# One decoder layer, MLA and NSA side by side: compression results in score banks, wo's splits and key pairs in the first attention, group norm gains in wo's split

## The chip, the cores and the metric

The kernel runs on one core of a Trainium2 chip. The metric is the time of one execution on the device in microseconds, the median of several runs. All times of a trace come from one profiled execution.

## What is computed

One layer for 512 positions of width 1024, in float32. After an RMS norm, one projection feeds two attentions, and both outputs go, each with its own RMS norm, through one matrix; then a squared-ReLU feed-forward part.

```python
h = rms_norm(x, ln1_g)
h_q, h_kv, h_kr, q_b, kv_b, gate_b = split(h @ w_in)
o_a = mla_mixer(...)      # 8 heads, causal, 512 keys, low-rank q and kv
# nsa_mixer: 8 heads, 2 kv heads, three branches with sigmoid gates
k_cmp = rms_norm(silu(blocks_k @ w1) @ w2, k_gain[0])   # 31 blocks of 32 positions
v_cmp = silu(blocks_v @ w1) @ w2
o_b = g0 * o_cmp + g1 * o_sel + g2 * o_win              # sel takes all 8 key blocks here
mix = concat([rms_norm(o_a, grp_norm_mla), rms_norm(o_b, grp_norm_nsa)])
x = x + mix @ w_o
h2 = rms_norm(x, ln2_g)
x = x + square(relu(h2 @ w_up)) @ w_down
```

## The kernel before

**Precision.** Dense products run as three matmuls of a faster 32-bit form: each operand is split into a rounded part and the rest (`hi`, `lo`), and hi·hi, hi·lo and lo·hi are added in PSUM. A weight piece is 128 x 1024; SyncE loads it into one of three `raw` buffers, ScalarE writes `w_hi` (L608), VectorE writes `w_lo = raw - w_hi` (L927). Both live in a ring of five. A raw buffer is free when its `w_lo` is written (`raw_free`), a ring slot when its last product has run. The order of the pieces is a list, `weight_pieces`: eight pieces of wo, the first five ahead of the four of `w1`, which are not split.

**Units.** Positions come in four tiles of 128, t = 0 to 3. An attention unit is one tile of queries of one head: scores (`score_unit`, two score banks `S`), minimum and subtraction on VectorE (`low_unit`, L1087), the exponential on ScalarE (L741), 128x128 turns by TensorE into one of two `T` banks (L1454), a copy out by ScalarE for even units and VectorE for odd ones (`pt_out`, L751 and L1097), and the product with the values (`mix_unit`, L1640). TensorE's order in step n is: scores of n, filling work, product of n-4, turn of n-2. The first attention has 32 units, n = 0 to 31; the second counts u = n - 32: sel 3 (u 0 to 7), win 3 (8 to 15), sel 2 (16 to 23), win 2 (24 to 31), cmp 3 (32), sel 1 (33 to 40), cmp 2 (41), win 1 (42 to 49), cmp 1 (50), sel 0, win 0, cmp 0 (67). A compression unit holds all eight heads.

**Filling work.** In the first attention: 32 projection pieces for the second attention's keys, values and gates, spread by `unit_of`, and the norms of its queries and keys (`NORM_AT`: squares on ScalarE, sums and two products on VectorE, turns). In the second, `compress(u)` of each engine: at u 0 to 9 the key taps, gates and bias are turned; at u 10 to 17 the hidden layer of the compression; at u 21, 23 and 27 its second products `kc` and `vc` and the turn of `kc`, which go into `T` banks, between the turns of the probabilities. `take` hands out the two banks of a kind in turn and makes TensorE wait until the user two before has been read. Mixed rows of the first attention (`mix_row_of` on GpSimd: norm factor, then gain row L563) are turned at u 19, 21, 23 and 25 and split by ScalarE and VectorE in the two units after. From u 28 on the products with wo (`WO_UNITS`) fill TensorE.

**What sets the order.** Each engine works its program strictly in order, and the positions are written out by hand: `WO_SPLIT` says in which unit of the second attention each piece of wo is split (4, 6, 7, 9, 9, 44, 45, 46), `PAIR_KEYS` and `PAIR_QUERIES` when keys and queries are put into hi/lo pairs (`pair_his`, `pair_los`), `X_AGAIN` after which piece SyncE loads x again. The keys of tile 3 are paired in the step after the first attention's last scores, ahead of its last output row. An output row (`out_row`) divides a branch's eight heads by their sums; the mix of the branch two later waits for it, as both share a bank `O`.

## Time and profile before

| | us |
|---|---|
| median of 3 runs | 725.37 (724.8 to 729.68) |
| the profiled execution | 724.78, span 722.5 |
| TensorE busy, of the span | 691.0 |
| VectorE busy | 366.6 |
| ScalarE busy | 292.8 |
| GpSimd busy | 107.6 |
| stages: input projections | 0 to 103 |
| first attention | 103 to 190 |
| second attention and wo | 190 to 378 |
| feed-forward | 378 to 722.5 |

A profile page names the engines PE (TensorE), DVE (VectorE), ACT (ScalarE), POOL (GpSimd) and SP (SyncE). A row of windows gives a stretch of time and its length, then how long each engine was busy in it, with its number of instructions, in the order TensorE's matmuls, TensorE's weight loads (beside the matmuls), VectorE, ScalarE, GpSimd; then the clock that TensorE was granted (1.00 is 2.4 GHz, 0.50 is 1.2 GHz), the share of the DMA engines and GB/s. A row of a group gives line, engine, operation, output and inputs with their shapes, how often, then the busy time in us and the mean of one in ns. A row of waits says which instruction's end released an engine that stood idle. A busy TensorE at half clock shows as busy.

### The profile page before, as it was taken

To read this page: it belongs to the slowest core of one execution; us is meant where nothing else is said; L and a number is where in the kernel's file an instruction comes from. 1 tells how busy PE (TensorE), PEld (TensorE's weight loads), DVE (VectorE), ACT (ScalarE), POOL (GpSimd) and SP (SyncE) were. 2 spreads that over 40 slices of the span, in tenths; PEclk is the share of its full clock that TensorE was granted. 3 is DMA by queue.
4 is the path that set the end of the run, shared out by engine and by line. 5 is a ranking of instruction groups with operands and counts; after the bars stand their busy time and mean duration, and the time that the engine had idled before them with its cause. 6 is when DMAs were issued, how large, how long until landed. Compare 5 with 4: busy or idle time off the path is not lost.

```text
span 722.5 us, 9978 instructions
## 1 busy us (share of the span) xinstructions
PE 691.0 (96%) x3703; PEld 590.8 (82%) x3703; DVE 366.6 (51%) x713; ACT 292.8 (41%) x630; POOL 107.6 (15%) x152
## 2 busy tenths in 40 slices
PE   7999999999899799898799999999999999999998
PEld 5989877888689788787699888888888888888886
DVE  4645665777685764767655454323224445432311
ACT  5554665556674542645244343321122343321110
POOL 2526654310240300224100000000000000000000
PEclk9999999999999899989999999999999999999999
DMA  7331314100245000020033322322322322322302
GB/s 281 115 130 33 117 61 149 62 27 2 88 154 206 22 1 0 15 74 31 1 117 100 104 88 94 110 88 96 109 88 88 115 89 87 114 91 88 103 1 102
DMA packets 18529, 62.14 MB, mean 86 GB/s; under 512 B 2184, under 2 KB 2312, under 8 KB 18482
## 3 DMA queue, kind: packets, MB, share of 16 engines
q1 hardware_dynamic: 17138, 57.50, 23.7%
q0 software_dynamic: 1200, 3.94, 1.7%
q8 instruction: 30, 0.49, 0.3%
q14 instruction: 17, 0.14, 0.1%
q10 hardware_dynamic: 144, 0.07, 0.0%
HBM read 59.35 MB, written 2.15 MB: 85 GB/s over the span
## 4 chain that ended last, share of the span: by engine, by line
PE 84%; DVE 7%; issue 3%; ACT 3%; DMA 1%; POOL 1%; SPq 0%; DVEq 0%; ACTq 0%; POOLq 0%
PE bank L1433 14%; PE bank L1435 14%; PE bank L1434 14%; PE bank L1756 8%; PE bank L1755 8%; PE bank L1754 8%; PE bank L1454 6%; PE bank L1640 5%; PE bank L1601 2%; PE bank L1682 1%; DVE w_lo L927 1%; DVE s_buf L1087 1%; DMA x<-x 1%; PE bank L1613 1%; PE bank L1612 1%
## 5 line engine op out<-in xcount | busy, mean ns | idle before, releaser
L927 DVE TENSOR_TENSOR w_lo<-raw,w_hi 128x1024 fp32r<-128x1024 f32 (+3 forms) x97 | 113.5, 1175 | 122.7 <-ACT w_hi L608 122.5
L608 ACT ACTIVATE w_hi<-raw 128x1024 fp32r<-128x1024 f32 (+3 forms) x97 | 97.5, 1011 | 122.5 <-PE bank L1435 118.2
L1754 PE MATMUL bank<-act_hi,w_hi 128*128 128x512 f32 (+3 forms) x288 | 106.8, 371 | 0.0
L1756 PE MATMUL bank<-act_hi,w_lo 128*128 128x512 f32 (+3 forms) x288 | 106.7, 370 | 0.0
L1755 PE MATMUL bank<-act_lo,w_hi 128*128 128x512 f32 (+3 forms) x288 | 106.7, 370 | 0.0
L1433 PE MATMUL bank<-w_hi,a_hi 128*128 128x512 f32 x256 | 99.6, 389 | 0.0
L1434 PE MATMUL bank<-w_lo,a_hi 128*128 128x512 f32 x256 | 99.6, 389 | 0.0
L1435 PE MATMUL bank<-w_hi,a_lo 128*128 128x512 f32 x256 | 99.6, 389 | 0.0
L1433 PE MATMUL bank<-w_hi,act_hi 128*128 128x512 f32 (+3 forms) x224 | 92.3, 412 | 2.5 <-DVE act_lo L940 2.3
L1434 PE MATMUL bank<-w_lo,act_hi 128*128 128x512 f32 (+3 forms) x224 | 81.4, 363 | 0.0
L1435 PE MATMUL bank<-w_hi,act_lo 128*128 128x512 f32 (+3 forms) x224 | 81.0, 362 | 0.0
L741 ACT ACTIVATE p_buf<-s_buf,stats 128x128 f32<-128x128 f32 (+3 forms) x96 | 53.5, 558 | 45.0 <-PE bank L1454 36.1
L1398 DVE TENSOR_TENSOR sq_b<-relu_b 128x512 f32<-128x512 f32 x32 | 22.1, 692 | 82.0 <-ACT relu_b L912 82.0
L912 ACT ACTIVATE relu_b<-bank 128x512 f32<-128x512 f32 x32 | 19.1, 598 | 106.3 <-PE bank L1756 106.3
L1755 PEld LDWEIGHTS bank<-act_lo,w_hi 128*128 128x128 f32 x288 | 54.2, 188 | 9.2
L1754 PEld LDWEIGHTS bank<-act_hi,w_hi 128*128 128x128 f32 x288 | 54.2, 188 | 9.0
L1756 PEld LDWEIGHTS bank<-act_hi,w_lo 128*128 128x128 f32 x288 | 54.2, 188 | 9.0
L1434 PEld LDWEIGHTS bank<-w_lo,a_hi 128*128 128x128 f32 x256 | 48.1, 188 | 10.0
L1433 PEld LDWEIGHTS bank<-w_hi,a_hi 128*128 128x128 f32 x256 | 48.1, 188 | 10.0
L1435 PEld LDWEIGHTS bank<-w_hi,a_lo 128*128 128x128 f32 x256 | 48.1, 188 | 9.9
L1433 PEld LDWEIGHTS bank<-w_hi,act_hi 128*128 128x128 f32 x224 | 43.4, 194 | 11.7 <-DVE act_lo L940 2.8
L1454 PE MATMUL bank<-consts,p_buf 128*128 128x128 f32 x248 | 45.7, 283 | 7.3 <-DVE kc_row L1310 3.5
(193 smaller groups left out, 1062.5 us busy)
## 6 DMA issues: line engine op xcount, KB each, us to landing
raw<-weights SPq DMA_DIRECT2D x86, 512.0 KB, 3.3
x<-x SPq DMA_DIRECT2D x8, 512.0 KB, 7.0
raw<-weights SPq DMA_DIRECT2D x7, 384.0 KB, 4.4
bias<-bias_by_distance POOLq DMA_DIRECT2D x1, 2048.0 KB, 9.1
y<-x SPq DMA_DIRECT2D x8, 256.0 KB, 2.2
raw<-weights SPq DMA_DIRECT2D x4, 288.0 KB, 2.8
raw<-weights SPq DMA_DIRECT2D x4, 280.0 KB, 3.0
consts<-consts SPq DMA_DIRECT2D x1, 688.0 KB, 4.1
```

The source lines that it names most:

```text
L608: act.activation(w_hi[:, m % RING, 0:width], raw[:, n % RAW, 0:width], ACT.Copy).then_inc(*hi_done.mark(n))
L741: act.activation(p_buf[:, n % 2, 0:nk], s_buf[:, n % 2, 0:nk], ACT.Exp, scale=-1.0, bias=neg_max[:, m:m + 1], accum_out=den[:, d:d + 1]).t ...
L927: dve.tensor_tensor(w_lo[:, m % RING, 0:width], raw[:, n % RAW, 0:width], w_hi[:, m % RING, 0:width].bitcast(F32), ALU.subtract).then_inc( ...
L1398: dve.tensor_tensor(sq_b[:, f % 2, :], relu_b[:, f % 2, :], relu_b[:, f % 2, :], ALU.mult).then_inc(*sq_done.mark((half, f)))
L1433: pe.matmul(dst, a_h, w_h, start=start, stop=False)
L1434: pe.matmul(dst, a_h, w_l, start=False, stop=False)
L1435: return pe.matmul(dst, a_l, w_h, start=False, stop=stop)
L1454: ins = pe.transpose(bank[0:m, i * step:i * step + k], tile, ident[0:k, 0:k])
L1640: ins = pe.matmul(bank[:, 64 * h:64 * h + 64], pt_buf[:, n % 2, j * P:(j + 1) * P], v, start=j == 0, stop=j == t)
L1754: pe.matmul(dst, h[:, ws], act_hi[:, k, cols], start=k == 0, stop=False)
L1755: pe.matmul(dst, h[:, ws], act_lo[:, k, cols], start=False, stop=False)
L1756: ins = pe.matmul(dst, l[:, ws], act_hi[:, k, cols], start=False, stop=k == KD - 1)
```

## The change

1. The weights' order: three pieces of wo ahead of w1, the other five behind; x is loaded again after the last piece of w1.
2. The splits of wo: pieces 0, 1, 2 in units 17, 27, 30 of the first attention; 3 to 7 at u 20, 29, 38, 40, 42.
3. The projection pieces of the first attention end two to three units sooner, so that the keys of tile 3 are paired at unit 29; query norms come at units 9, 16, 19, 22. The last query pair moves from u 43 to u 46.
4. The second products of the compression go into columns 384 to 511 of score bank `S[1]`, which units 16 to 31 leave free, ahead of the scores of u 19, 27 and 25; the score unit two later waits until VectorE has read them. `vc` is made once, for 32 rows, and copied to four places.
5. Mixed rows of the first attention are turned at u 9, 15, 20, 23. GpSimd norms the fourth after the compressed key's norm factor.
6. The gains of both group norms are multiplied into wo when it is split, as a scale per partition: each split is two ScalarE and two VectorE instructions of 512 columns. The gain rows, their load and the gain pass go.
7. Four tiles are zeroed by GpSimd before its eight loads of `tap_planes`, not by VectorE at u 6.

```diff
-    add("wo", RING, 1024)
+    add("wo", 3, 1024)
     add("w1", 4, 1024, False)
-    add("wo", 8, 1024, first=RING)
+    add("wo", 8, 1024, first=3)
...
-X_AGAIN = PIECE_AT["w1", 2]
+X_AGAIN = PIECE_AT["w1", 3]
...
-WO_SPLIT = {0: 4, 1: 6, 2: 7, 3: 9, 4: 9, 5: 44, 6: 45, 7: 46}
+WO_SPLIT = {0: 17 - N_MLA, 1: 27 - N_MLA, 2: 30 - N_MLA, 3: 20, 4: 29, 5: 38, 6: 40, 7: 42}
...
-    return 2 + (4 * row + piece_) * 30 // 32
+    return 2 + (4 * row + piece_) * 27 // 32
...
-NORM_AT = {ROW_END[0]: ("nkv", 0), 6: ("nq", 3), ROW_END[1]: ("nkv", 1), 10: ("nq", 2), ROW_END[2]: ("nkv", 2),
-           14: ("nq", 1), ROW_END[3]: ("nkv", 3), 19: ("nq", 0)}
+NORM_AT = {ROW_END[0]: ("nkv", 0), ROW_END[1]: ("nkv", 1), 9: ("nq", 3), ROW_END[2]: ("nkv", 2), ROW_END[3]: ("nkv", 3),
+           16: ("nq", 2), 19: ("nq", 1), 22: ("nq", 0)}
...
-PAIR_QUERIES = {25: 3, N_MLA + 13: 2, N_MLA + 23: 1, N_MLA + 43: 0}
+PAIR_QUERIES = {25: 3, N_MLA + 13: 2, N_MLA + 23: 1, N_MLA + 46: 0}
...
+MIX_AT = {9: 0, 15: 1, 20: 2, 23: 3}
+KC_AT, VC_AT, KT_AT = 19, 27, 25
+TAIL = 3 * P
+TAIL_READ = {KC_AT: "kc0", VC_AT: ("vd", 3), KT_AT: "k_cmp"}
...
+            pool.memset(v_diag, 0.0)
+            pool.memset(hid_v, 0.0)
+            pool.memset(hid_k, 0.0)
+            pool.memset(k_cmp, 0.0).then_inc(*pool_step.mark("zeros"))
             for h in range(HEADS):
...
-            for t in range(NT):
+            for t in range(3):
                 mix_row_of(0, t)
-            sum_branches("win", 3)
             pool.wait_ge(*dve_step.at("kc_ss"))
             rsqrt("kc", kc_rs[0:64, :], kc_ss[0:64, :], HD)
-            sum_branches("win", 2)
+            mix_row_of(0, 3)
+            for t in (3, 2):
+                sum_branches("win", t)
...
+                if PIECES[n][0] == "wo":
+                    for j, gain in enumerate(group_gains(n)):
+                        cols = slice(512 * j, 512 * j + 512)
+                        ins = dve.scalar_tensor_tensor(w_lo[:, m % RING, cols], raw[:, n % RAW, cols], gain,
+                                                       w_hi[:, m % RING, cols].bitcast(F32), ALU.mult, ALU.subtract)
...
-                        for g in range(2):
-                            rep = lambda v: v[:, g, :].unsqueeze(1).to_broadcast([P, 4, N_CMP])
-                            dve.tensor_tensor(hid_v[:, g, :, 0:N_CMP], rep(z), rep(r), ALU.mult).then_inc(*dve_step.mark(("hid_v", g)))
+                        dve.tensor_tensor(hid_v[:, :, 0:N_CMP], z, r, ALU.mult).then_inc(*dve_step.mark("hid_v"))
...
+                if u == KT_AT - 1:
+                    dve.wait_ge(*rsqrt_done.at("kc"))
+                    dve.scalar_tensor_tensor(kc_sq, kc_row, kc_rs[0:64, :], const("g_nk", 64)[:, 0:HD], ALU.mult, ALU.mult).then_inc(*dve_step.mark("kc2"))
...
+            def compress_tail(u):
+
+                if u == KC_AT:
+                    pe.wait_ge(*dve_step.at("hid_k"))
+                    pe.matmul(S[1][0:64, TAIL:TAIL + HD], hid_k, const("w2")[:, 0:HD], start=True, stop=True).then_inc(*turned.mark("kc"))
+                if u == VC_AT:
+                    pe.wait_ge(*dve_step.at("hid_v"))
+                    for g in range(2):
+                        ins = pe.matmul(S[1][0:NC, TAIL + g * HD:TAIL + (g + 1) * HD], hid_v[:, g, :], const("w2")[:, HD:], start=True, stop=True)
+                    ins.then_inc(*turned.mark("vc"))
+                if u == KT_AT:
+                    pe.wait_ge(*dve_step.at("kc2"))
+                    pe.transpose(S[1][0:64, TAIL:TAIL + 64], kc_sq, ident[0:64, 0:64]).then_inc(*turned.mark("kcT"))
...
+                if n - 2 - N_MLA in TAIL_READ:
+                    pe.wait_ge(*dve_step.at(TAIL_READ[n - 2 - N_MLA]))
+                compress_tail(n - N_MLA)
```

## Rows read from the trace of the kernel before

**Rows 1.** Windows by stage: length, busy us (count) per engine, granted clock, DMA.

```profile
145.00:190.00 45.00, 43.19 (x309) 37.31 (x308) 31.08 (x83) 25.36 (x66) 3.06 (x5) 1.00 0.02 9
190.00:212.00 22.00, 18.67 (x134) 15.16 (x133) 20.52 (x46) 18.27 (x42) 11.62 (x18) 1.00 0.45 145
236.00:262.00 26.00, 20.89 (x142) 19.57 (x141) 19.28 (x54) 13.90 (x36) 6.67 (x9) 0.87 0.00 1
300.00:316.00 16.00, 12.35 (x63) 10.39 (x63) 11.90 (x33) 9.66 (x24) 4.97 (x5) 0.79 0.25 81
378.00:722.50 344.50, 341.27 (x1544) 283.92 (x1543) 123.49 (x139) 94.66 (x123) 0.00 (x0) 1.00 0.28 92
```

**Rows 2.** Windows around the three longest stops, columns as before.

```profile
242.30:245.80 3.50, 0.03 (x1) 0.03 (x1) 3.47 (x8) 0.36 (x1) 1.54 (x2) 0.86 0.00 0
245.80:251.20 5.40, 5.40 (x25) 5.40 (x26) 1.92 (x6) 3.23 (x7) 0.72 (x2) 0.50 0.00 0
303.20:306.80 3.60, 0.39 (x5) 0.21 (x3) 3.31 (x9) 2.83 (x7) 0.00 (x0) 0.93 0.18 46
306.80:313.10 6.30, 6.30 (x22) 5.55 (x23) 3.04 (x9) 1.94 (x5) 2.15 (x4) 0.50 0.40 143
346.90:350.80 3.90, 1.29 (x12) 1.13 (x11) 2.52 (x4) 1.09 (x2) 0.00 (x0) 0.98 0.02 4
350.80:354.20 3.40, 3.40 (x8) 2.73 (x9) 3.15 (x10) 0.00 (x0) 0.00 (x0) 0.52 0.00 0
```

**Rows 3.** Waits of TensorE, 190 to 212: total us, times, longest.

```profile
PE bank L1454 <- DVE tap_planes L1251: 2.5, 3, 1.2
...
PE bank L1682 <- DMA raw<-weights: 0.5, 1, 0.5
```

**Rows 4.** Waits of TensorE, 236 to 262.

```profile
PE bank L1454 <- DVE kc_row L1310: 3.5, 1, 3.5
PE bank L1454 <- DVE v_diag L1320: 1.1, 1, 1.1
PE bank L1454 <- DVE k_cmp L1328: 0.6, 1, 0.6
```

**Rows 5.** Waits of TensorE, 300 to 316.

```profile
PE bank L1640 <- DVE o_nsa L1123: 3.2, 1, 3.2
```

**Rows 6.** VectorE's groups of instructions, 190 to 212: busy us, mean ns.

```profile
L927 DVE TENSOR_TENSOR w_lo<-raw,w_hi 128x1024 fp32r<-128x1024 f32 x5 | 6.3, 1281 | 0.0
...
L1271 DVE MEMSET v_diag<- 128x512 f32 x1 | 0.5, 485 | 0.1
```

**Rows 7.** VectorE in order of time, units 20 to 24: start, length.

```profile
238.44 0.55 DVE L1087 CUSTOM_DVE_ANT_0 s_buf<-bank,bias 128x384 f32<-128x384 f32 x1
...
238.91 0.17 DVE L1108 TENSOR_SCALAR stats<-stats 128x8 f32<-128x8 f32 x1
...
239.55 0.69 DVE L1131 TENSOR_TENSOR raw_row<-bank,stats 128x512 f32<-128x512 f32 x1
...
240.63 0.64 DVE L1293 TENSOR_SCALAR z_buf<-z_buf 128x62 f32<-128x62 f32 x1
...
241.88 2.11 DVE L1304 TENSOR_TENSOR hid_v<-z_buf 128x124 f32<-128x124 f32 x2
...
253.16 0.69 DVE L1211 TENSOR_TENSOR q_pairs<-n_q,q_pairs 64x512 fp32r<-64x512 f32 x1
```

**Rows 8.** TensorE in order of time: first score products of two units.

```profile
237.68 0.42 PE L1612 MATMUL bank<-act_hi,q_pairs 128*128 128x384 f32 x1
...
238.98 0.42 PE L1612 MATMUL bank<-act_hi,q_pairs 128*128 128x384 f32 x1
```

**Rows 9.** VectorE's groups, 103 to 190, by shape: key pairs.

```profile
L1203 DVE TENSOR_TENSOR act_lo<-n_k,act_hi 64x256 fp32r<-64x256 f32 x16 | 6.6, 415 | 0.2
```

**Rows 10.** GpSimd's groups, 103 to 380: gain of the mixed rows.

```profile
L563 POOL TENSOR_TENSOR mix_row<-mix_row,gain_grp 128x512 f32<-128x512 f32 x7 | 9.8, 1398 | 0.6
```

**Rows 11.** VectorE in order of time: last mixed row.

```profile
358.04 0.75 DVE L1378 SCALAR_TENSOR_TENSOR mix_row<-o_nsa,stats,gain_grp 128x512 f32<-128x512 f32 x1 [1.10 <-POOL stats L465]
```

More of the change, by code:

```diff
@@ L313, in build @@
         r_mv = r_mk + 16384
-        gain_grp = place("gain_grp", D_MODEL, at=r_mv)
         gain_ln2 = place("gain_ln2", D_MODEL, at=r_nk)
@@ L1258, in compress @@
             def compress(u):
+                if u == KC_AT:
+                    dve.wait_ge(*turned.at("kc"))
+                    dve.tensor_copy(kc_row, S[1][0:64, TAIL:TAIL + HD]).then_inc(*dve_step.mark("kc0"))
+                    dve.wait_ge(*dve_step.at("kc0"))
+                    dve.tensor_tensor(kc_sq, kc_row, kc_row, ALU.mult).then_inc(*dve_step.mark("kc1"))
+                    dve.wait_ge(*dve_step.at("kc1"))
+                    dve.tensor_reduce(kc_ss[0:64, :], kc_sq, AX.X, ALU.add).then_inc(*dve_step.mark("kc_ss"))
+                if u == VC_AT:
+                    dve.wait_ge(*turned.at("vc"))
+                    for h in range(4):
+                        ps = slice(32 * h, 32 * h + 32)
+                        dve.tensor_copy(v_diag[ps, :, HD * h:HD * h + HD],
+                                        S[1][0:NC, TAIL:TAIL + 2 * HD].rearrange("p (g n) -> p g n", g=2)).then_inc(*dve_step.mark(("vd", h)))
+                if u == KT_AT - 1:
+                    dve.wait_ge(*rsqrt_done.at("kc"))
+                    dve.scalar_tensor_tensor(kc_sq, kc_row, kc_rs[0:64, :], const("g_nk", 64)[:, 0:HD], ALU.mult, ALU.mult).then_inc(*dve_step.mark("kc2"))
+                if u == KT_AT:
+                    dve.wait_ge(*turned.at("kcT"))
+                    dve.tensor_copy(k_cmp[0:64, 0:NC], S[1][0:64, TAIL:TAIL + NC]).then_inc(*dve_step.mark("k0"))
+                    dve.tensor_copy(k_cmp[64:128, NC:2 * NC], S[1][0:64, TAIL + NC:TAIL + 2 * NC]).then_inc(*dve_step.mark("k_cmp"))
                 if u in (1, 3, 5, 7):
@@ L1315, in compress @@
-                if u == 24:
-                    dve.wait_ge(*turned.at("vc"))
-                    bank = TD[bank_of("T", "vc")]
-                    for h in range(4):
-                        ps = slice(32 * h, 32 * h + 32)
-                        dve.tensor_copy(v_diag[ps, :, HD * h:HD * h + HD], bank[ps, 0:2 * HD].rearrange("p (g n) -> p g n", g=2)).then_inc(*dve_step.mark(("vd", h)))
-                if u == 26:
-                    dve.wait_ge(*rsqrt_done.at("kc"))
-                    dve.scalar_tensor_tensor(kc_sq, kc_row, kc_rs[0:64, :], const("g_nk", 64)[:, 0:HD], ALU.mult, ALU.mult).then_inc(*dve_step.mark("kc2"))
@@ L1377, in _ @@
             dve.wait_ge(*turned.at(("mix", 1, 2)))
-            dve.scalar_tensor_tensor(mix_row[:, 1, :], o_nsa[:, 0, :], rs_mix[:, NT:NT + 1], gain_grp[:, 512:1024],
-                                     ALU.mult, ALU.mult).then_inc(*mixed_last.mark())
+            dve.tensor_scalar(mix_row[:, 1, :], o_nsa[:, 0, :], rs_mix[:, NT:NT + 1], None, ALU.mult).then_inc(*mixed_last.mark())
             ln2_rows(1)
@@ L1712, in compress @@
                     hidden((u - 10) // 4, (u - 10) % 4)
-                if u == 21:
-                    pe.wait_ge(*dve_step.at("hid_k"))
-                    bank = take("T", "kc", (dve_step, "kc0"))
-                    pe.matmul(bank[0:64, 0:HD], hid_k, const("w2")[:, 0:HD], start=True, stop=True).then_inc(*turned.mark("kc"))
-                if u == 23:
-                    pe.wait_ge(*dve_step.at(("hid_v", 1)))
-                    bank = take("T", "vc", (dve_step, ("vd", 3)))
-                    for g in range(2):
-                        ins = pe.matmul(bank[:, g * HD:(g + 1) * HD], hid_v[:, g, :, :].rearrange("p h c -> p (h c)"), const("w2")[:, HD:], start=True, stop=True)
-                    ins.then_inc(*turned.mark("vc"))
-                if u in (19, 21, 23, 25):
-                    turn_mix(0, (u - 19) // 2)
-                if u == 27:
-                    pe.wait_ge(*dve_step.at("kc2"))
-                    turn("kcT", [kc_sq], (dve_step, "k_cmp"))
+                if u in MIX_AT:
+                    turn_mix(0, MIX_AT[u])
             def project_out(g, t, c, j):
```

70 lines of the change are left out of this document (30 added, 40 removed).

## The prediction, made before the changed kernel ran

> **What bounds the kernel now.** I read the windows of the stages first, then the waits of TensorE inside the stages where it has idle time, then the order of time around the two longest stops. From 378 us on TensorE is busy in 341.27 of 344.50 us at full clock [rows 1]: the feed-forward part is bound by its matmuls, and the change leaves its work alone, so it is a constant of 344.5. Time can only come from the two attentions between 103 and 378. There the windows show TensorE idle for 1.81 us of 145 to 190, 3.33 of 190 to 212, 5.11 of 236 to 262 and 3.65 of 300 to 316 [rows 1], and in the last two the granted clock averages 0.87 and 0.79. The finer windows tell why: TensorE is nearly empty for 3.50 us from 242.3, and the next 5.40 us run at 0.50; it is nearly empty for 3.60 us from 303.2, and 6.30 us at 0.50 follow; after 346.9, where 2.61 of 3.90 us are idle in several pieces, 3.40 us follow at 0.52 [rows 2]. Matmuls at 1.2 instead of 2.4 GHz do half the work, so the first two falls cost 5.40/2 = 2.7 and 6.30/2 = 3.15 us on top of the idle time. In both empty stretches VectorE is busy throughout (3.47 of 3.50, 3.31 of 3.60) [rows 2]: TensorE waits on a full VectorE queue. The whole prize is 3.33 + (5.11 + 2.7) + (3.65 + 3.15) = 17.9 us, and 1.8 in the first attention.
>
> **The change part by part, u = unit counted from the second attention's first.**
>
> *First attention, 103 to 190.* Projection pieces come in 27 units, not 30; TensorE's work is the same, only units 29 to 31 have none beside their scores. Into VectorE's queue of units 17 to 31 come three splits of wo (17, 27, 30), one more group-query norm and part of another, and the pair of keys 3 with its gates (which the window to 190 holds already). A split is now two scalar_tensor_tensor of 512 columns in place of one pass of 1024. None of that form is in the trace; the one of 128x512 on the last mixed row took 0.75 [rows 11], an ordinary 512-column pass 0.69 [rows 7], the present split 1.28 [rows 6]: between 1.28 and 1.50, I take 1.38. Three make 4.1. A query norm is four passes of 0.69 = 2.8 [rows 7]; the part of the second is 0.7; pieces moved ahead give back about 1.5. VectorE's 31.08 busy of 45.00 us [rows 1] becomes about 31.1 + 4.1 + 2.8 + 0.7 - 1.5 = 37.2, or 83%. At 93% (20.52 of 22.00, the next row) TensorE lost 3.33 us in 22. So 83% should pass except where it bunches: unit 30 has a score pass and a copy of 0.69 each, the key pair's four passes of 0.415 [rows 9] and a split, 1.4 + 1.7 + 1.4 = 4.5 us, while TensorE's mean unit in this window is 43.19/16.5 = 2.6 us [rows 1], and without its projection piece an estimated 2.2. Some 1.3 us of stop at the end of the first attention replace what is idle there now, about 0.9, and the 0.9 that unit 21 costs now goes. I take 0; worst -3 (one stop above 3 us or two shorter), best +1.8. ScalarE gets three splits and the pair, about 6 us on 25.36 of 45.00: hidden.
>
> *Second attention, u 0 to 9 (190 to 212).* VectorE loses five splits, 5 x 1.28 = 6.4 us [rows 6], and four memsets, of which the largest is 0.49 [rows 6], together 0.97: 7.4 of 20.52. The named waits of TensorE here are VectorE's tap copies, 2.5 us in 3, and 0.5 for the piece w1, that is now loaded before the first attention ends [rows 3]. The first tap wait hangs on ScalarE's exponentials and copies, which are as before. I leave 1.0 of 3.33: gain 2.3. Least 0.5 (w1's wait alone), most 3.3. The memsets go to GpSimd ahead of its eight loads of the tap planes' bias. No memset on GpSimd is in the trace; from nothing to twice VectorE's 0.97. The loads are needed at u 7, about 12 us after they are issued, so even 2 us are covered; behind them stands only the first mixed row, whose input comes at u 6.
>
> *u 18 to 28 (236 to 262).* Now VectorE has at u 21 the two replicated products (2.11 us), a tensor_scalar that took 0.64 and a reciprocal, after an output row from 238.91 to 240.24 [rows 7]; TensorE stands at the next turn, since the compression product has one of the two turning banks, until kc_row is read: 3.5 us; the same happens with v_diag (1.1) and k_cmp (0.6) [rows 4]. The change puts these three results in the free columns of score bank S[1], so a turn waits for none of them, and makes one small product of the two. But three score units now wait: u 25 stands behind the scaled key row, which VectorE makes in u 24. I walk that: from the scores of u 20, VectorE has five score passes of 0.55, three copies of 0.55, an output row of 1.33, wo piece 3 at 1.38, the silu at about 1.1, one mixed low of 0.69 and the key row at 0.3: 2.75 + 1.65 + 1.33 + 1.38 + 1.1 + 0.69 + 0.3 = 9.2 us. TensorE's units start 1.30 apart (237.68, 238.98) [rows 8]; five less the score already done, and two turns of a mixed row, make 6.5 - 0.3 + 1.1 = 7.3. It stands about 2 us, spread or at u 25; I leave 2.2 of 5.11 idle and no fall of the clock: gain 2.9 + 2.7 = 5.6. Worst: 3.5 idle and a fall as now, gain 1.6; best 7.8. Mixed rows 0 and 1 are turned at u 9 and 15, under 212 to 236, where VectorE has room.
>
> *u 42 to 46 (300 to 316).* TensorE waits 3.2 us for the output row of sel 1 [rows 5], which stands in VectorE's queue behind the query pair (two passes of 0.69 [rows 7]) and a split of 1.28, each begun late by ScalarE's half. Pair and splits move: pair to u 46, splits to 38, 40, 42. Ahead of the row are taken 1.38 + 1.28 and about 0.7 of waits, and one split of 1.38 comes: 2.0 less. I leave 2.1 idle, now in two places, so no fall: gain 1.55 + 3.15 = 4.7. Least 1.5, most 6.8. The pair is used at u 51, so it is not late.
>
> *Mixed rows.* GpSimd loses its gain pass, 1.4 us each, seven times [rows 10]; no TensorE wait names it. The last row's 0.75 becomes an ordinary 0.69: 0.1 at the end. Its 0.5 MB load goes, hidden before.
>
> *A rule about GpSimd.* The tensor_scalar of u 21 took 0.64 with 62 columns [rows 7] beside GpSimd's passes. The Trainium skill, "SBUF — State Buffer", section "SBUF: two separate sides", says that VectorE and GpSimd share a port pair under an exclusive lock, which a VectorE pass with two SBUF inputs needs too. By that rule the new split at u 20, with two SBUF inputs, could wait for GpSimd's sum of the window branch, and the sum would come out near 713.9 instead. The trace agrees in kind, but no row holds this pair of passes; the term above does not use it.
>
> **Sum.** 0 + 2.3 + 5.6 + 4.7 + 0.1 = 12.7. The profiled execution took 724.78 (span 722.5), so 712.1; the median is 0.59 above it: 712.7.
>
> **Rivals.**
> 1. *The clock still falls.* The two stops I leave (2.2 and 2.1) may be whole instead of spread; the fall after 346.9 came with only 2.61 idle [rows 2]. Against it: 190 to 212 has 3.33 idle in short pieces at clock 1.00 [rows 1]. Price: 2.7 + 1.3 for the first, 3.15 for the second: 716.7 with one, 719.9 with both. The Trainium skill, "TensorE: Matmul & The Clock Gate", section "A second HAM failure mode: psum-queue depth-cycling", also tells of small idles that lower the clock; the trace shows both outcomes. 0.18.
> 2. *All VectorE waits vanish* because passes overlap better than my walk: 712.7 - (1.0 + 2.2 + 2.1) - 1.8 = 705.6. 0.10.
> 3. *The first attention eats it.* VectorE at 83% with bursts stops TensorE for 6 us and nothing else goes wrong; net gain 6: 719. 0.09.
> 4. *Slower: units 17 to 31 become VectorE-bound.* If TensorE loses there what it lost at 93% (15% of 45 = 6.8) and the clock falls after each of the bursts at 20 to 23, 25 to 27 and 30 (3 x 2.9 = 8.7), the loss is 15.5: 728.2. It decides once the first attention loses more than 12.7. For it: VectorE's own work of units 17 to 31, by the same passes about 39 us, equals TensorE's 39; against it: it has several us of slack between a score and its use. 0.03.
>
> **How the numbers follow.** The forecast, 708 to 717, has 0.60. The range 706 to 720 takes in nearly all of rivals 1 to 3 and leaves out under 0.2. One per cent is about what a measurement of this kernel can tell from no change: below 718.1 lie the forecast, rival 2 and half of rival 1, 0.79; above 732.6 only several of the costs together, 0.02; the rest 0.19.
>
> **What would show it.** TensorE's waits list kc_row, v_diag and k_cmp with nearly nothing; 236 to 262 and 300 to 316 have clock near 1.00; 190 to 212 has under 1.5 idle; the splits' mean is near 0.69 per half; the clock's average over the span is above 0.99. Wrong it would be if TensorE stops over 3 us near unit 30, or at u 25, and the clock falls behind it.

## The result, and the profile after

| | before | after |
|---|---|---|
| median, us | 724.80 (723.69 to 729.68, 11 executions) | 721.28 (718.28 to 723.96, 11 executions) |
| profiled execution | 724.78, span 722.5 | 719.78, span 718.0 |
| ratio | | 0.9936, 95% interval 0.9917 to 0.9955 |

The change saves 3.5 us of the 12.7 that were predicted. The windows of the changed kernel by stage, columns as in [rows 1]:

```profile
145.00:190.00 45.00, 42.00 (x290) 35.55 (x290) 36.56 (x91) 29.48 (x74) 5.89 (x6) 0.98 0.11 36
190.00:212.00 22.00, 20.71 (x142) 17.76 (x142) 15.18 (x40) 12.98 (x34) 8.21 (x19) 0.89 0.18 48
236.00:262.00 26.00, 24.25 (x178) 21.82 (x177) 21.95 (x62) 16.70 (x42) 3.82 (x6) 1.00 0.13 42
300.00:316.00 16.00, 15.25 (x84) 13.06 (x83) 10.80 (x35) 7.80 (x23) 3.11 (x4) 0.79 0.10 34
378.00:718.00 340.00, 336.76 (x1508) 279.41 (x1507) 123.49 (x139) 94.20 (x123) 0.00 (x0) 1.00 0.28 93
```

And finer windows of the same kernel, around its two long stops:

```profile
184.00:188.00 4.00, 2.10 (x19) 1.87 (x19) 3.16 (x7) 1.77 (x5) 0.00 (x0) 1.00 0.18 59
188.00:195.00 7.00, 7.00 (x31) 6.37 (x31) 2.44 (x7) 0.53 (x1) 2.29 (x7) 0.51 0.13 47
...
286.00:301.00 15.00, 11.61 (x81) 9.93 (x80) 10.52 (x28) 8.81 (x24) 2.71 (x4) 0.99 0.22 71
301.00:307.40 6.40, 6.26 (x20) 5.14 (x21) 4.59 (x17) 3.71 (x10) 0.79 (x1) 0.50 0.26 84
```

Each stretch is priced as in the prediction, as idle time plus half of the time at half clock:

- 145 to 190: idle 3.00, it was 1.81 [rows 1]. 1.2 worse.
- 190 to 212: idle 1.29, it was 3.33: 2.0 better. But 188 to 195 runs at 0.51, where the kernel before has no fall: 7.00 x 0.49 = 3.4 worse.
- 236 to 262: idle 1.75 at full clock; it was 5.11 and a fall worth 2.7 [rows 1, 2]. 6.1 better.
- units 38 to 46: idle 3.39 from 286 to 301 and 0.14 behind it, with 6.40 us at half clock worth 3.2, 6.7 in all. Before it was 3.65 + 3.15 = 6.8, in another place. 0.1 better.

Together -1.2 + 2.0 - 3.4 + 6.1 + 0.1 = 3.6 us; 316 to 378, with 6.19 us idle where the kernel before has 6.75, gives 0.6 more. That is 4.2, against 4.5 between the two spans. So one stop went as forecast, one came at the end of the first attention, and one only moved. The totals of the two profiles say the same without an estimate, as TensorE's work is nearly the same in both: it is busy for 691.0 us of 722.5 before and for 691.4 of 718.0 after. The change took away 4.9 us of waiting, and nothing of what the falls of the clock cost.

**The new stop.** VectorE in order of time at the end of the first attention (start, length, line, operation):

```profile
182.23 0.68 DVE L1110 CUSTOM_DVE_ANT_0 s_buf<-bank,consts 128x512 f32<-128x512 f32 x1
182.83 0.08 DVE L1110 DVE_READ_ACCUMULATOR2_ANT stats<- 128x1 f32 x1
182.83 1.72 DVE L1226 TENSOR_TENSOR act_lo<-n_k,act_hi 64x256 fp32r<-64x256 f32 x4
184.58 1.41 DVE L946 SCALAR_TENSOR_TENSOR w_lo<-raw,consts,w_hi 128x512 fp32r<-128x512 f32 x2
185.91 0.68 DVE L1110 CUSTOM_DVE_ANT_0 s_buf<-bank,consts 128x512 f32<-128x512 f32 x1
186.52 0.08 DVE L1110 DVE_READ_ACCUMULATOR2_ANT stats<- 128x1 f32 x1
186.52 0.69 DVE L1120 COPY pt_buf<-bank 128x512 f32<-128x512 f32 x1
```

and TensorE's next product:

```profile
187.26 1.22 PE L1668 MATMUL bank<-m_v,pt_buf 128*128 128x64 f32 x8 [1.90 <-DVE pt_buf L1120]
```

The pair of keys 3 (1.72) and the split of wo's piece 2 (1.41) stand one behind the other, so the copy of the turned probabilities is 3.1 us late. This is the bunch of unit 30 that the prediction walked through; it called its stop 1.3 us, and it was 1.9.

**The stop that moved.** ScalarE in order of time around unit 38, in the changed kernel:

```profile
287.88 0.63 ACT L854 ACTIVATE square<-o_nsa 128x512 f32<-128x512 f32 x1 [4.16 <-POOL o_nsa L582]
...
288.51 0.49 ACT L759 ACTIVATE p_buf<-s_buf,stats 128x256 f32<-128x256 f32 x1
...
289.00 1.32 ACT L623 ACTIVATE w_hi<-raw,consts 128x512 fp32r<-128x512 f32 x2
290.23 0.36 ACT L769 ACTIVATE pt_buf<-bank 128x256 f32<-128x256 f32 x1
```

ScalarE stands 4.16 us before the square of a compression row, which waits for GpSimd's sum; its exponential and its copy come late, and the split goes ahead of the copy. TensorE's waits from 286 to 302 (total, times, longest) are five small ones, 3.4 us in all:

```profile
PE bank L1668 <- ACT pt_buf L769: 1.2, 2, 0.8
PE bank L1668 <- DVE pt_buf L1120: 1.0, 1, 1.0
PE bank L1633 <- DVE stats L1110: 0.6, 1, 0.6
PE bank L1640 <- DVE stats L1110: 0.6, 1, 0.6
```

None is over 1.01 us, and the clock falls behind them all the same.

ScalarE's stop of 4.16 us is not new. It stands before the same square in the kernel before, and in e9 (below), which has no split from u 30 to 41:

```profile
292.28 0.63 ACT L836 ACTIVATE square<-o_nsa 128x512 f32<-128x512 f32 x1 [3.91 <-POOL o_nsa L570]
```

```profile
283.17 0.63 ACT L854 ACTIVATE square<-o_nsa 128x512 f32<-128x512 f32 x1 [4.17 <-POOL o_nsa L582]
```

In neither does TensorE wait at this place: its next wait comes at 302.9 before and at 292.5 in e9. So what made the five waits is the splits that were put behind ScalarE's late start.

**What varies between executions.** Each execution gives a span and a mean granted clock. Span x clock is roughly the length that the same work and waits would have at full clock; the rest, span x (1 - clock), is roughly what the falls cost. For the kernels of this study, the median of the first and the median and range of the second:

| kernel | executions | median us | span x clock | lost to the clock |
|---|---|---|---|---|
| before (all its executions beside the experiments) | 44 | 724.9 | 713.2 | 8.7 (6.5 to 16.8) |
| changed | 11 | 721.3 | 709.3 | 10.1 (7.2 to 13.7) |
| e1, piece 2 at 28 | 4 | 715.2 | 709.8 | 3.6 (3.6 to 5.0) |
| e9 and e9b, all pieces spread | 10 | 712.2, 711.9 | 708.3, 707.8 | 2.1 (0.7 to 7.1) |
| e15, gains on GpSimd | 4 | 710.5 | 705.7 | 2.5 (0.7 to 4.3) |

By these medians the change took 3.9 us of waits away and paid 1.4 more to the clock. Most of what moving single pieces gains or loses below stands in the last column. That column puts a fall too high, since TensorE also stands idle in part of one: in e15 it goes from 0.7 to 4.3 us while the spans stay within 0.8 us of each other, and in e13 from 0.7 to 8.6 for spans that are 4.7 apart. So the two columns are a guide to within a few us, not a sum.

In the profiled executions of all these kernels, each fall between 103 and 378 costs about 1.7 us or about 3.4 us of full clock. The kernel before has three (3.4, 3.4 and 1.7), the changed kernel three (3.4, 3.4 and 1.7), e9 one and e15 none.

### The profile page after: what moved, and what is told of

It reads as the page before. It is cut to its first block, busy times and chain, and to the rows that moved or that the text cites. A ratio compares the mean times of both kernels' runs of the same rounds, so it can differ in the third digit from the quotient of the medians.

```text
span 718.0 us, 9987 instructions
## 1 busy us (share of the span) xinstructions
PE 691.4 (96%) x3703; PEld 590.0 (82%) x3703; DVE 365.8 (51%) x716; ACT 294.8 (41%) x638; POOL 96.5 (13%) x148
## 4 chain that ended last, share of the span: by engine, by line
PE 84%; DVE 7%; ACT 3%; issue 3%; DMA 1%; POOL 0%; SPq 0%; DVEq 0%; ACTq 0%; POOLq 0%
PE bank L1444 14%; PE bank L1445 14%; PE bank L1446 14%; PE bank L1771 8%; PE bank L1770 8%; PE bank L1769 8%; PE bank L1465 5%; PE bank L1668 5%; PE bank L1710 1%; PE bank L1629 1%; DVE s_buf L1110 1%; PE bank L1640 1%; PE bank L1641 1%; DVE w_lo L946 1%; DMA x<-x 1%
## 5 line engine op out<-in xcount | busy, mean ns | idle before, releaser
L949 DVE TENSOR_TENSOR w_lo<-raw,w_hi 128x1024 fp32r<-128x1024 f32 (+3 forms) x89 | 103.4, 1167 | 119.5 <-ACT w_hi L625 119.4
L625 ACT ACTIVATE w_hi<-raw 128x1024 fp32r<-128x1024 f32 (+3 forms) x89 | 89.1, 1008 | 122.7 <-PE bank L1446 119.1
L1444 PE MATMUL bank<-w_hi,act_hi 128*128 128x512 f32 (+3 forms) x224 | 90.2, 403 | 2.4 <-DVE act_lo L963 2.1
L1668 PE MATMUL bank<-n_v,pt_buf 128*128 128x64 f32 x320 | 45.3, 273 | 4.2 <-ACT pt_buf L769 2.4
```

What stands on the lines that cost most here:

```text
L625: ins = act.activation(w_hi[:, m % RING, 0:width], raw[:, n % RAW, 0:width], ACT.Copy)
L949: ins = dve.tensor_tensor(w_lo[:, m % RING, 0:width], raw[:, n % RAW, 0:width], w_hi[:, m % RING, 0:width].bitcast(F32), ALU.subtract)
L1444: pe.matmul(dst, a_h, w_h, start=start, stop=False)
L1668: ins = pe.matmul(bank[:, 64 * h:64 * h + 64], pt_buf[:, n % 2, j * P:(j + 1) * P], v, start=j == 0, stop=j == t)
```

## The experiments

Each kernel is named by its label. "The spread kernel" is e9.

### e1, e2, e3: where the splits stand

```diff
-WO_SPLIT = {..., 2: 30 - N_MLA, 3: 20, 4: 29, 5: 38, 6: 40, 7: 42}
+WO_SPLIT = {..., 2: 28 - N_MLA, 3: 20, 4: 29, 5: 38, 6: 40, 7: 42}   e1
+WO_SPLIT = {..., 2: 30 - N_MLA, 3: 20, 4: 29, 5: 38, 6: 45, 7: 49}   e2
+WO_SPLIT = {..., 2: 28 - N_MLA, 3: 20, 4: 29, 5: 38, 6: 45, 7: 49}   e3
```

> The changed kernel with one number altered: piece 2 of wo is split at unit 28 of the first attention instead of unit 30, where VectorE already has key pair 3 (1.72 us), the split (1.41 us) and the low half in a row. Theory 1 (the bunch at unit 30 stops TensorE for about 1.9 us at 187.3 and its clock then falls for some 7 us): no idle of TensorE over 0.5 us between 180 and 190, clock near 1.00 from 188 to 200, the second attention's first score near 189 instead of 192.4, and the kernel 3 to 5 us shorter than the changed one, 717 to 718 against 721.3. Theory 2 (key pair 3 at unit 30 alone is enough for the stop): the wait stays over 1 us and the time stays within 1 us of the changed kernel. Theory 3 (the fall comes at some place anyway, whichever wait begins it): the wait goes, another fall of 5 to 7 us shows up between 190 and 260, time within 1 us of the changed kernel.

Measured: 715.24 (714.62 to 716.67), ratio 0.9831 [0.9776, 0.9886]. The first two windows of e1:

```profile
145.00:190.00 45.00, 43.16 (x307) 36.78 (x306) 37.44 (x94) 30.12 (x75) 5.92 (x7) 1.00 0.11 36
190.00:212.00 22.00, 20.41 (x151) 17.29 (x151) 15.94 (x40) 14.86 (x40) 9.43 (x22) 1.00 0.17 48
```

Idle from 145 to 190 is 1.84 again, as before the change, with the same work in VectorE's queue (37.44 us, the estimate was 37.2). The first theory holds for the stop and its fall: one number, two units, 6.0 us, more than the 3 to 5 that I expected. Of the wait 0.7 us is left, behind key pair 3 alone. In this execution, the slowest of the four, the clock fell for some 4 us after 244, behind 1.5 us of idle, and again after 298 and 343; so part of the third theory holds too.

> The changed kernel with the late pieces of wo split at units 38, 45 and 49 instead of 38, 40 and 42, so that units 39 to 43, which are short, carry one split less. Theory 1 (ScalarE's 1.32 us half and VectorE's 1.41 us half in units of 1.1 us are what makes the waits of 288 to 302): idle of TensorE there falls from about 3.5 us to under 1.5, the clock stays near 1.00 from 295 to 310, last compressed score 3 to 5 us earlier, kernel 717 to 718.5. Theory 2 (what is left is the output of mla and the score banks, the o_nsa wait of before in another dress, not the splits): idle stays over 2.5 us and the fall stays; time within 1 us of the changed kernel. Theory 3 (the splits at 45 and 49 make a new stop in the third heads' units): waits on hi, lo or pt buffers behind unit 45, and the time is 1 us or more above the changed kernel.

Measured: 717.73 (716.64 to 719.03). In the profiled execution 286 to 316 has 3.47 us of idle, as much as the changed kernel's 3.5, and a clock of 1.00: the idle time stayed and the fall went, which neither theory had. 3.5 us faster, all of it in the clock. The waits are not the same ones. With the split still at u 38, two of the changed kernel's five stay:

```profile
291.61 0.66 PE L1668 MATMUL bank<-n_v,pt_buf 128*128 128x64 f32 x4 [0.82 <-ACT pt_buf L769]
293.13 1.10 PE L1633 MATMUL bank<-k_cmp,n_q 128*128 128x64 f32 x8 [0.59 <-DVE stats L1110]
```

The other three (1.01, 0.38 and 0.59), which came behind the split of u 40, are gone; 0.44 at 301.8 and 1.27 at 307.8 came instead. In e9, with no split at u 38 either, these two are gone as well.

> Both moves at once: wo's piece 2 at unit 28, its late pieces at units 38, 45 and 49. If the two stops are independent and are where the expected gain went, the sum of the two single gains, 6 to 9 us under the changed kernel, 712 to 715.5. If the clock falls at some later place whatever is moved, one of the two gains is lost again and it is 717 to 719. If neither is the cause, 720 to 722.

Measured: 713.39, 718.50, 719.27 and 725.08, median 718.89. The gains did not add: span x clock is 709.2 and nearly all of the difference between these four is in the clock, whose mean was 0.997, 0.990, 0.988 and 0.979. Its profiled execution has a fall at 244 to 251, one near 293 and one near 310. Inconclusive on its own; what it shows is that with idle pieces of 1 to 2 us left in three places the falls are not the same from one execution to the next.

### e8, e9 and e9b: piece 3 away from GpSimd's sum, then the late ones

```diff
+WO_SPLIT = {..., 2: 28 - N_MLA, 3: 26, 4: 29, 5: 38, 6: 40, 7: 42}   e8
+WO_SPLIT = {..., 2: 28 - N_MLA, 3: 26, 4: 29, 5: 42, 6: 45, 7: 49}   e9
```

In the changed kernel the split at u 20 took twice its time, beside GpSimd's sum of the window branch. VectorE and GpSimd of the changed kernel, in order of time:

```profile
242.21 2.71 DVE L946 SCALAR_TENSOR_TENSOR w_lo<-raw,consts,w_hi 128x512 fp32r<-128x512 f32 x2
```

```profile
242.67 1.71 POOL L582 TENSOR_TENSOR o_nsa<-o_nsa,raw_row 128x512 f32<-128x512 f32 x1
```

> The first experiment's kernel (piece 2 of wo at unit 28) with wo's piece 3 split at unit 26 of the second attention instead of 20, where its two VectorE instructions took 2.72 us beside GpSimd's window sum of 1.71 us. Theory 1 (the two hold each other up, and that is the 1.1 us stats wait at 240 from which the clock falls): the two instructions take 1.4 us, the sum 1.3 us, the wait of 1.1 us goes, no fall at 244, and the kernel is 1.5 to 3.5 us under the first experiment's 715.2, that is 711.7 to 713.7. Theory 2 (VectorE's work at unit 20 is simply too long, the neighbour on GpSimd does nothing): the split still takes 2.7 us at unit 26. Theory 3: the split at 26 meets v_diag's copies at 27 and makes a wait of its own of 1 us or more there; 714.5 to 716.

Measured: 713.74 (713.23 to 717.27), 1.5 us under e1 by the medians, with ranges that overlap (e1 714.62 to 716.67). The halves of e8's splits after 236 take 0.75 us each, the stats wait of 1.1 us at 240 is gone, 236 to 262 has 0.51 idle and clock 1.00. The run e4 below holds the same split at the same unit 20, where GpSimd's sum came 5 us after it, so the unit is not what made it long:

```profile
241.85 1.40 DVE L945 SCALAR_TENSOR_TENSOR w_lo<-raw,consts,w_hi 128x512 fp32r<-128x512 f32 x2
```

```profile
247.10 1.27 POOL L582 TENSOR_TENSOR o_nsa<-o_nsa,raw_row 128x512 f32<-128x512 f32 x1
```

2.71 + 1.71 beside each other, 1.40 + 1.27 apart: 1.75 us lost by standing together. The Trainium skill, "SBUF — State Buffer", section "SBUF: two separate sides", says that a VectorE pass with two SBUF inputs and a GpSimd pass that reads SBUF exclude each other for whole instructions. The trace agrees: 0.70 + 1.27 + 0.70 = 2.67, the half split, the sum and the other half one behind the other, is near the 2.71. It agrees twice more: the query pair's pass at u 46 took 1.61 us beside a sum and 0.68 without one (e9 and e12), and the product for `hid_v` 0.78 beside GpSimd's gain pass and 0.23 without (e6b and the changed kernel). The prediction put the price of it at 713.9 - 712.7 = 1.2 us. Moving the split took the idle time of 236 to 262 from 1.50 in e1 to 0.51; the 1.5 us between the medians is less certain, for the overlap.

> As the kernel with pieces 2 and 3 of wo moved (units 28 and 26), and its late pieces at units 42, 45 and 49: none in units 37 to 41, where ScalarE stands behind GpSimd's sum. If the bunch of units 38 to 42 is still worth its 2 us of idle and a fall of the clock: 1 to 3 us under the kernel with pieces 2 and 3 moved alone, 709.5 to 712. If the late units are as tight, as the runs with 38, 45 and 49 left open (their times lay between 713.4 and 725): waits move to 300 to 310 and the time is within 1 us of it or above.

Measured: 712.22 (711.85 to 712.46), 1.5 us under e8, all four executions within 0.6 us. By the two columns this step is all in the clock: span x clock is 707.8 in e8 and 708.3 here, the cost of the clock 4.3 and 2.1.

> The spread kernel (pieces of wo split at unit 28 of the first attention and units 26, 29, 42, 45, 49 of the second) once more, in more rounds, for the interval of its ratio to the kernel before and as the base of the other runs of this call. Expected 711.8 to 712.8, ratio 0.981 to 0.983, mean granted clock of each execution 0.995 or more, as in its first round. If that round was luck and the clock falls in some executions as in the changed kernel: several at 715 and above.

Measured: 711.86 (710.61 to 715.26), ratio 0.9823 [0.9795, 0.9850]. Its windows, in e9:

```profile
145.00:190.00 45.00, 43.16 (x307) 36.73 (x306) 37.40 (x95) 30.08 (x74) 5.95 (x7) 1.00 0.11 36
190.00:212.00 22.00, 20.42 (x152) 17.31 (x151) 15.93 (x40) 14.89 (x40) 9.45 (x22) 1.00 0.16 49
236.00:262.00 26.00, 25.48 (x183) 23.15 (x183) 22.06 (x63) 16.38 (x42) 3.40 (x6) 1.00 0.14 42
286.00:316.00 30.00, 27.11 (x175) 23.70 (x174) 23.38 (x69) 16.62 (x49) 4.09 (x5) 0.94 0.16 53
```

With the change's parts as they are and five numbers of one table altered, the kernel takes 712. That this is the predicted time is chance, as the places are not those of the prediction. Two executions of e9b were at 713.8 and 715.3: the falls became rare, not impossible.

### e14: unit 30 in the spread kernel

`2: 30 - N_MLA` in e9.

> The spread kernel with piece 2 of wo back at unit 30 of the first attention, where the changed kernel has it. In the changed kernel the move to 28 was worth 6.0 us (721.3 to 715.2), of which 1.2 us is idle time in the first attention and 3.4 the fall behind it. Theory 1 (stop of 1.9 us and fall belong to unit 30 whatever comes later): 4 to 6 us slower than the spread kernel, 716.2 to 718.2, with the clock at half from about 189 to 195. Theory 2 (the fall depends on later stops): 713 to 714.5.

Measured: 715.28 (714.71 to 716.47), 3.4 us above e9b, which ran beside it, and between the ranges of the two theories. The stop of 1.9 us at 187 is back, yet this time nothing falls behind it, and the profiled execution falls at 330 and 340 instead. The windows of e14:

```profile
184.00:188.00 4.00, 2.11 (x18) 1.87 (x18) 3.32 (x7) 1.84 (x5) 0.00 (x0) 1.00 0.21 59
188.00:195.00 7.00, 6.61 (x47) 5.23 (x47) 4.41 (x13) 2.75 (x8) 4.08 (x11) 1.00 0.25 85
```

Against the changed kernel's two windows above, TensorE did the same in the four microseconds before (2.10 and 2.11 busy), and was granted 0.51 there and 1.00 here. The program is also the same in both up to u 20, long after this stop. Four profiled executions hold that same beginning (the changed kernel, e2, e4 and e14), and the clock fell behind the stop in three of them. In none of the profiled executions without the stop did it fall there. So the stop is needed for this fall, but the rows around it do not tell whether the fall comes. What decided it is open.

### e4 and e10: the compression products back in the turn banks

```diff
-    pe.matmul(S[1][0:64, TAIL:TAIL + HD], hid_k, ...)        # ahead of the scores of u 19
+    bank = take("T", "kc", (dve_step, "kc0"))                # u 21, read at 22
+    pe.matmul(bank[0:64, 0:HD], hid_k, ...)
...
```

The same for `vc` (u 23, read at 24) and the turn of `kc` (27, read at 28); e4 from the changed kernel, e10 from the spread one. In both, GpSimd's norm of the fourth mixed row also goes back ahead of the compressed key's.

> The changed kernel with the compression products back in the turn banks, made at units 21, 23 and 27 and read at 22, 24 and 28 as before the change; everything else as changed. Theory 1 (the score-bank columns are what took away the stops of units 20 to 27, 3.7 us of idle and a fall of the clock): the waits on kc_row, v_diag and k_cmp come back, with the fall, and the kernel is 4 to 6.5 us slower than the changed one, 725.5 to 728. Theory 2 (the splits taken out of these units by the change are what removed the stop; the banks do little): less than 1.5 us slower, 721 to 723, with waits on the products under 1 us in all.

Measured: 721.92 (719.72 to 723.02), 0.6 above the changed kernel, where I had expected 4 to 6.5. The waits did come back, 1.8 on kc_row, 1.3 on v_diag, 0.6 on k_cmp, and span x clock rose by 2.7. The clock cost 8.6 instead of 10.1 and hid about half of it. The time is that of the second theory, the waits are those of the first.

> The kernel with wo's pieces spread (28 in the first attention; 26, 29, 42, 45, 49 in the second), and the compression products back in the turn banks. In the changed kernel itself that move cost only 0.6 us. Theory 1 (the banks are worth what the prediction gave them, 5.6 us, but other stops hid it in the changed kernel, by luck of where the clock fell): waits of 3 to 4 us between 236 and 262 with a fall behind them, 5 to 7 us slower than the spread kernel's 712.2, 717.5 to 719. Theory 2 (the banks are worth their waits, 2 to 2.5 us, and no more): 714 to 715.5.

Measured: 714.82 (713.45 to 714.97), 2.6 above e9; the stretch in e10:

```profile
236.00:262.00 26.00, 22.80 (x163) 20.38 (x162) 20.11 (x58) 14.86 (x37) 1.96 (x3) 1.00 0.13 42
```

3.20 idle against 0.52: 2.7 us of waits and no fall. The second theory holds: in the spread kernel the columns of the score bank are worth their waits and no more.

### e6 and e6b: that part alone, on the kernel before

The three products in `S[1]` as in the change, with the one small product for `hid_v`; splits, mixed rows, key pairs and gains as before.

> The kernel before with one part of the change alone: the three compression products into the free columns of the second score bank, made and read at the units of the change (with the single product for hid_v that goes with it). Splits, mixed rows, key pairs, group norm as before. Theory 1 (the turn banks are the stop of units 20 to 27, as the prediction's 5.6 us for this stretch say): TensorE's 5.1 us of idle between 236 and 262 falls to about 2 and the fall of its clock there goes; 4.5 to 6 us under the kernel before, 719 to 720.5. Theory 2 (what the run with the turn banks put back says: the banks give their waits, about 2.1 to 2.5 us, and a fall of the clock begins there in some executions with either): 1.5 to 3 us under, 722 to 723.5. Theory 3 (VectorE's and GpSimd's order at units 19 to 21 is what counts): within 1 us of before.

> The same kernel as the one with the compression products in the score bank alone, once more, for its profile: in the first round its other executions took 716.4 to 718.6 where the kernel before took 724.3. Expected again 716.5 to 719. If the score-bank columns take away the whole stop of units 20 to 27: under 1.2 us of idle of TensorE from 236 to 262 and no fall of the clock there, with the waits of 190 to 212 (3.3 us) and the o_nsa wait of units 42 to 46 (3.2 us) still there. If the gain comes from elsewhere: idle over 2 us in 236 to 262.

Measured: 717.69 (716.42 to 718.61) and 717.27 (716.48 to 718.03), ratios 0.9887 [0.9846, 0.9928] and 0.9872 [0.9833, 0.9910]. One further execution of e6 took 2,397 us, at a granted clock of 1.00, with matmuls of 128x512 that took 1.02 to 1.10 us where the kernel before has 0.37 to 0.39; I don't know why and leave it out. The stretch in e6b:

```profile
236.00:262.00 26.00, 25.36 (x191) 23.44 (x190) 20.89 (x61) 15.40 (x41) 6.64 (x9) 1.00 0.00 1
```

Idle 0.64 instead of 5.11, no fall: 4.5 + 2.7 = 7.2 by the trace, and by the medians 6.7 and 8.2 under the kernel before beside it (724.34 and 725.49). This part alone beats the whole change by 3.6 to 4.0 us. It does more here than in e10, since the kernel before also turns its mixed rows in these units and makes the 2.11 us products [rows 7]; with the turn banks each of those is one more user ahead of the next turn. The 2.11 us products, one behind the other from 241.88, also stand beside GpSimd's gain pass and its sum (241.31 to 243.84), and the one product of e6b takes 0.78. How much each of these adds is not tested by itself.

### e7 and e11: the five first pieces where they were

```diff
+WO_SPLIT = {0: 4, 1: 6, 2: 7, 3: 9, 4: 9, 5: 44, 6: 45, 7: 46}   e7, on the changed kernel
+WO_SPLIT = {0: 4, 1: 6, 2: 7, 3: 9, 4: 9, 5: 42, 6: 45, 7: 49}   e11, on the spread kernel
```

Both load five pieces ahead of w1, as before the change.

> The changed kernel with wo's pieces loaded and split where they were before the change (five pieces ahead of w1, splits at units 4, 6, 7, 9, 9, 44, 45 and 46); banks, mixed rows and group norm as changed. If the moved splits gain in sum (units 0 to 9 relieved by 2.3 us, the rest free, as predicted): 2 to 3 us slower than the changed kernel, 723.5 to 724.5, with waits of 2.5 us in units 4 to 9 and the o_nsa wait of about 3 us near 304. If the moved splits gave back in the first attention and at units 38 to 42 what they took from units 0 to 9 and 44 to 46: within 1 us of the changed kernel. If they cost more than they took, as the first experiment lets one think (the piece at unit 30 alone was worth 6 us): 2 to 4 us faster than the changed kernel, 717 to 719.

Measured: 721.83 (719.39 to 725.06), 0.5 above the changed kernel: the moves of all eight splits, as the change made them, are worth nothing. 236 to 262 has 0.50 idle here, and the o_nsa wait of 2.5 us is back.

> The spread kernel with the five first pieces of wo where they were before the change: loaded ahead of w1 and split at units 4, 6, 7, 9 and 9; the late ones at 42, 45 and 49. Theory 1 (the prediction's term for units 0 to 9): 2.3 us of idle more between 190 and 212, some 1 to 1.2 less in 236 to 262 and in the first attention together, so 0.8 to 1.5 us slower than the spread kernel, 713 to 713.7, if the clock keeps up there; 715 to 716.5 if the 3.9 us of idle between 200 and 210 let it fall. Theory 2 (VectorE's places for five splits are worth nothing): within 0.5 us of 712.2.

Measured: 714.24 (713.75 to 716.20), 2.0 to 2.4 above e9 and e9b. The windows of e11:

```profile
145.00:190.00 45.00, 43.54 (x309) 37.11 (x307) 34.08 (x88) 26.20 (x68) 6.53 (x11) 1.00 0.01 1
190.00:212.00 22.00, 18.14 (x133) 15.02 (x133) 19.77 (x45) 19.82 (x47) 7.20 (x15) 1.00 0.39 120
```

Idle 3.86 against 1.58 in 190 to 212, 0.38 less in the first attention. The time is a little above the first theory's 713 to 713.7. And e7 against e11 is the price of the places 44, 45 and 46 alone: 7.6 us, with nothing else different in the program. They did not run beside each other; by the two columns 6.5 of it is the clock (8.6 against 2.1).

### e12, e13: the stop that is left at unit 46

```diff
-                done = n - 5
+                done = n - 6      # ScalarE's square of a compression row, e12 and e13
-PAIR_QUERIES = {..., N_MLA + 46: 0}
+PAIR_QUERIES = {..., N_MLA + 48: 0}      e12 only
```

> The spread kernel with two more moves: ScalarE's square of a compression row one unit later, so that its exponentials and copies don't stand behind GpSimd's sum (ScalarE idle 2.54 us, then TensorE's 1.28 us stop at 300.2), and the last query pair at unit 48 instead of 46, where one of its passes took 1.61 us beside GpSimd's sum in place of 0.69. If ScalarE's wait is the cause of the stop at unit 46 and of that at unit 38: both go, no fall of the clock after 300, 1.5 to 3 us faster than the spread kernel, 709.2 to 710.7. If it is not: within 1 us of 712.2, with the stops where they were. If the turn of the mixed row then comes too late: a new wait on mix_row at units 40 to 42, over 1 us, and 712.5 to 714.

> The spread kernel with ScalarE's square of a compression row one unit later and nothing else (the query pair stays at unit 46; with it at 48 VectorE's bunch of pair and split made a new stop of 1.9 us). If ScalarE's wait behind GpSimd's sum causes the stop of 1.28 us at unit 46: that wait goes, none comes, and 0.8 to 2 us less than the spread kernel, 710.2 to 711.4. If VectorE's queue is as late as ScalarE's there: the wait changes its name and is 711.8 to 713.5.

Measured: e12 713.82 (713.39 to 716.98), e13 711.68 (710.66 to 715.38) beside e9b's 711.86. TensorE's only wait from 299 to 303, first in e9, then in e13:

```profile
PE bank L1668 <- ACT pt_buf L769: 1.3, 1, 1.3
```

```profile
PE bank L1668 <- DVE pt_buf L1120: 1.7, 1, 1.7
```

My guess fell: the wait changes its name. VectorE's queue, with the query pair of 1.61 us beside GpSimd's sum, is as late as ScalarE's. With the pair two units on (e12) its pass takes 0.68, but it then meets the split of u 49, for a stop of 1.9 us.

### e15: the group norm gains back on GpSimd

```diff
-                if PIECES[n][0] == "wo":      # two scaled halves in ScalarE and VectorE
+                # every piece: one plain pass of 1024 in each
+                pool.tensor_tensor(mix_row[...], mix_row[...], gain_grp[:, 512 * g:512 * g + 512], ALU.mult)
```

With the load of the gain rows and the old form of the last mixed row; all else as e9.

> The spread kernel with the group norm gains back on GpSimd: one pass of 1.4 us for each mixed row, the gain rows loaded again, and each split of wo one ScalarE and one VectorE instruction of 1024 columns (1.04 and 1.28 us instead of 1.32 and 1.41). Prediction's step: 0.1 us slower at the end and nothing elsewhere, 712 to 713. If the longer halves are what makes the late bunches: faster, 710.5 to 711.7. If GpSimd's extra passes delay the sums for which ScalarE waits at units 38 and 46, or take VectorE's port: 713 to 716, with passes of VectorE stretched beside them.

Measured: 710.46 (710.22 to 710.57), ratio 0.9794 [0.9762, 0.9826]. 1.4 us under e9b, which ran beside it, and the best kernel of the study. VectorE's and ScalarE's groups in it (170 to 310, busy us, mean ns):

```profile
L954 DVE TENSOR_TENSOR w_lo<-raw,w_hi 128x1024 fp32r<-128x1024 f32 x7 | 8.5, 1220 | 1.3 <-ACT w_hi L630 1.3
```

```profile
L630 ACT ACTIVATE w_hi<-raw 128x1024 fp32r<-128x1024 f32 x7 | 7.3, 1045 | 0.0
```

1.22 and 1.05 where the scaled halves take 1.41 and 1.32. In 286 to 316 TensorE is busy for 27.77 us (27.11 in e9, 26.93 in e9b), in 236 to 262 for 25.90 (25.48 and 25.50), and no fall is left in its profile. GpSimd's seven passes cost nothing, as nothing waited for them. So part 6 of the change moved free work of an idle engine onto the two whose queues make the stops named here. Whether the scale or the cut into halves makes the pair of passes longer was not separated.

## Why the prediction was wrong, by its own steps

- **Units 18 to 28**, forecast 5.6 (1.6 to 7.8): 6.1 in the changed kernel, 7.2 with the part alone. Right in the time and in the mechanism, but what is left agrees in part by luck. 1.75 us stay idle where I left 2.2, yet only 0.26 of it stands at u 25, where the walk put it. The largest wait, 1.14 before the scores of u 23, is the doubled time of the split at u 20, which the side sentence had priced and the sum had not used; without it 0.51 is left (e8), so the walk was too long.
- **Units 0 to 9**, forecast 2.3 (0.5 to 3.3): 2.0 by the windows, 2.0 to 2.4 by e11. Right; one tap wait of 1.2 us stayed. GpSimd's four memsets took 0.52 and three times 0.15, within the bounds, and nobody waited.
- **First attention**, forecast 0 (-3 to +1.8): -4.6. This is the first step that failed. The walk found the bunch and was off by 0.6 in the stop, which at 1.9 us is also under the "over 3 us" that I had named as the sign of being wrong. The mistake is in what it priced: every stop of [rows 2] was charged with the fall behind it, but this new one only with its idle time. Stop 1.2 net and fall 3.4 make 4.6. The share of 83% was right (it measured 81%) and told nothing; the stop sits in one unit.
- **Units 42 to 46**, forecast 4.7 (1.5 to 6.8): 0.1. The second step that failed. I priced what the row of sel 1 was rid of and not what stands at the places to which the splits went. Units 38 to 42 are the short ones, with 256 keys, and ScalarE comes into them late, after standing 4.16 us for GpSimd's sum. It did so before the change too (3.91), where nothing of TensorE hung on it; the splits put behind it made the five waits. "ScalarE" does not stand in that step. Against the old places, though, the new ones are no loss: 44, 45 and 46 cost 7.6 us more than 42, 45 and 49 (e7 and e11), 38, 40 and 42 only 1.5 more (e8 and e9).
- **"I leave 2.1 idle, now in two places, so no fall"**: the reason that both stretches shared, taken from 190 to 212 with its 3.33 idle at clock 1.00. It does not hold: five waits of at most 1.01 us were followed by a fall, and e14 has a stop of 1.9 us without one. The first rival had this mechanism, with 0.18, and a second place for it. The Trainium skill, "TensorE: Matmul & The Clock Gate", section "A second HAM failure mode: psum-queue depth-cycling", tells of a kernel in which frequent short idles made the clock go to and fro. The changed kernel agrees (6.40 us at 0.50 behind the five waits); e2, with 3.47 us idle in the same stretch at 1.00, shows that it need not come.
- **Mixed rows**, forecast 0.1 gain: a loss of 1.4 (e15). The split's length was right (1.38 forecast, 1.41 measured), but each of eight splits is 0.19 us longer on VectorE and 0.27 on ScalarE than the plain one (1.22 and 1.05 in e15). The walks used the VectorE length, against 1.28 for the plain one; ScalarE's had no term, and no step asked what the longer splits cost as a part of their own. The loss was measured in the spread kernel only.
- The third rival, the first attention eating the gain at 719, named one of the two places; its price is near the measured one by luck, as it comes from 6 us of stops and nothing else wrong, and the trace has one stop of 1.9 us with its fall and a second loss at u 38 to 42. The first rival's 719.9, with both falls of the second attention, is nearer to 721.28, but one of its two falls did not come.

The range failed with them: it reached to 720, both falls of the second attention, and left out a fall in a stretch that had none before.

## What to carry to other kernels

When work is moved, price the unit that it goes to as the one that it leaves: what stands ahead of it in each queue it enters, which of those passes wait for another engine, and which share a port with a pass beside them. Charge a new stop with the fall of the clock behind it as you do an old one, or at least put it into the range. Try each part by itself: one part alone, on the kernel before, beat all seven together by 3.6 to 4.0 us. And don't take work from an engine that is idle and that nobody waits for, if it goes to the one whose queue makes the stops.
